# Reordering the start of the expert units around the last row codes, with more filler between row codes, in a one-core hybrid layer kernel

## What is computed

```python
def hierarchical_moe(h, w_rg, b_rg, w_re, b_re, w_gate, w_up, w_down):
    # top-1 of 4 groups, then top-2 of the 4 experts in it
    grp_prob = softmax(t @ w_rg + b_rg);  grp_p, grp_idx = top_k(grp_prob, 1)
    in_group = the 4 logits (t @ w_re + b_re) of that group
    top_logits, top_local = top_k(in_group, 2)
    weights = grp_p * softmax(top_logits)
    expert_id = grp_idx * 4 + top_local
    out[t] = sum over the two experts e:
        weight_e * ((silu(t @ w_gate[e]) * (t @ w_up[e])) @ w_down[e])
```

## Time and profile before

| | us |
|---|---|
| median of 3 runs | 668.57 |
| lowest and highest | 668.28, 669.63 |
| profiled execution, its own time | 667.52 |
| its span in the profile | 665.8 |
| mean granted clock of TensorE in it | 0.986 |
| TensorE busy | 635.4 |
| VectorE busy | 477.3 |

### The profile page before, as it was taken

How to read it: one execution, slowest core, us unless ns; L and a number is a source line. 1 busy time by engine, 2 the same in 40 slices (tenths; PEclk the granted TensorE clock), 3 DMA queues, 4 the chain that set the end, 5 groups by cost and what they waited for, 6 DMA issues and landing times.

```text
span 665.8 us, 9330 instructions
## 1 busy us (share of the span) xinstructions
PE 635.4 (95%) x3396; PEld 525.9 (79%) x3397; DVE 477.3 (72%) x808; ACT 393.6 (59%) x670; POOL 171.3 (26%) x216
## 2 busy tenths in 40 slices
PE   7999999968899999999999998999999999999985
PEld 6788878756688898888888886788888888888863
DVE  5778995367622534425664658899999999999877
ACT  7448584246635142244342463388899888998753
POOL 7000007995000000000000000234747546556100
PEclk9999999998999999999999999799999999999998
DMA  9556535203422222222325954268687876985673
GB/s 279 189 168 191 128 80 156 66 6 79 128 64 64 64 63 64 64 64 74 116 67 202 388 195 159 56 199 276 207 284 242 277 278 219 295 260 174 234 272 127
DMA packets 76960, 108.51 MB, mean 163 GB/s; under 512 B 31863, under 2 KB 54464, under 8 KB 76786
## 3 DMA queue, kind: packets, MB, share of 16 engines
q1 hardware_dynamic: 64320, 99.76, 46.4%
q0 software_dynamic: 12480, 8.11, 4.1%
q10 hardware_dynamic: 114, 0.04, 0.0%
HBM read 123.90 MB, written 20.98 MB: 218 GB/s over the span
## 4 chain that ended last, share of the span: by engine, by line
PE 85%; DVE 8%; DMA 2%; ACT 2%; issue 1%; SPq 0%; POOLq 0%; DVEq 0%; ACTq 0%
PE bank L1748 22%; PE bank L1750 22%; PE bank L1749 22%; PE bank L2201 3%; DMA expert_rows<-expert_rows_hbm 1%; PE bank L1816 1%; PE bank L1998 1%; PE bank L1988 1%; DVE rank_onehot L1586 1%; ACT w_hi L810 1%; DVE probs L1319 1%; DVE y_T L1718 1%; PE bank L2119 1%; DMA x_T<-in_x 1%; PE bank L2217 1%
## 5 line engine op out<-in xcount | busy, mean ns | idle before, releaser
L1748 PE MATMUL bank<-h_hi,w_hi 128*128 128x512 f32 x288 | 117.7, 409 | 0.0
L1750 PE MATMUL bank<-h_hi,w_lo 128*128 128x512 f32 x288 | 113.0, 392 | 0.0
L1749 PE MATMUL bank<-h_lo,w_hi 128*128 128x512 f32 x288 | 112.7, 391 | 0.0
L1466 DVE TENSOR_TENSOR gate_up_lo<-ew_raw,gate_up_hi 128x1024 fp32r<-128x1024 f32 x92 | 108.4, 1218 | 1.8 <-ACT gate_up_hi L1018 1.8
L1135 DVE TENSOR_TENSOR w_lo<-w_raw,w_hi 128x2048 fp32r<-128x2048 f32 x26 | 59.8, 2300 | 52.1 <-ACT w_hi L810 52.1
L742 POOL DMA_INDIRECT unit_tokens<-ffn_rows,row_index x23 | 27.8, 1207 | 266.1 <-DVE row_index L1594 255.1
L1018 ACT ACTIVATE gate_up_hi<-ew_raw 128x1024 fp32r<-128x1024 f32 x92 | 92.1, 1051 | 0.9 <-DMA ew_raw<-in_w_up,extra_weight_rows 0.9
L1748 PE MATMUL bank<-gate_up_hi,unit_in_hi 128*128 128x512 f32 x184 | 75.9, 413 | 0.2 <-DVE unit_in_lo L1620 0.2
L1750 PE MATMUL bank<-gate_up_hi,unit_in_lo 128*128 128x512 f32 x184 | 72.1, 392 | 0.0
L1749 PE MATMUL bank<-gate_up_lo,unit_in_hi 128*128 128x512 f32 x184 | 71.9, 391 | 0.0
L1748 PEld LDWEIGHTS bank<-h_hi,w_hi 128*128 128x128 f32 x288 | 54.5, 189 | 12.0 <-issue 2.2
(11 more groups left out here) (396 smaller groups left out, 1300.3 us busy)
## 6 DMA issues: line engine op xcount, KB each, us to landing
w_raw<-in_w_in SPq DMA_DIRECT2D x16, 1024.0 KB, 5.2
ew_raw<-in_w_gate SPq DMA_DIRECT2D x32, 512.0 KB, 6.1
ew_raw<-in_w_up SPq DMA_DIRECT2D x32, 512.0 KB, 6.3
ew_raw<-in_w_down SPq DMA_DIRECT2D x32, 512.0 KB, 5.3
expert_rows_hbm<-sub_product SPq DMA_DIRECT2D x16, 256.0 KB
w_raw<-in_w_out SPq DMA_DIRECT2D x4, 1024.0 KB, 5.1
expert_rows<-expert_rows_hbm SPq DMA_DIRECT2D x8, 512.0 KB, 7.2
x_T<-in_x SPq DMA_DIRECT2D x4, 512.0 KB, 5.0
```

What stands on the lines that cost most here:

```text
L1466: dve.tensor_tensor(dst, eraw[slot][:, :], hi.bitcast(F32), ALU.subtract).then_inc(elo_done, 1)
L1748: pe.matmul(out_ap, lhs_hi, rhs_hi, start=first, stop=False)
L1749: pe.matmul(out_ap, lhs_hi, rhs_lo, start=False, stop=False)
L1750: return pe.matmul(out_ap, lhs_lo, rhs_hi, start=False, stop=last)
```

## The change

TensorE: the filler now stands between the row codes, six ahead of batch 0, six ahead of batch 1, two ahead of batch 2 and one ahead of batch 3 (with the twelve ahead of the rank counts the filler grows from 18 to 27 matmuls). The transposes of unit 0 come ahead of the row codes of batch 4, and the first half of unit 0's products comes ahead of the transposes of unit 1 and of that of the slot weights. VectorE: the low part of unit 0's rows comes ahead of the slot weights and of the row indices of batch 4; `extra_units` is cut in two, `extra_experts` (up to the weight rows) ahead of `split_in_lo(1)` and `extra_ranks` (with `one_hots(5)` at its end) after it. The instructions are otherwise the same, and ScalarE's, GpSimd's and SyncE's orders are not touched.

```diff
--- before.py
+++ after.py
@@ -452,6 +452,7 @@
             return ps[4 * ((j + 1) % 2) + r]
 
         EARLY = 5
+        GAP_FILL = (6, 6, 2, 1)
 
         def code_units(b):
 
@@ -1604,16 +1605,6 @@
             row_ids(2)
             one_hots(4)
             row_ids(3)
-            dve.wait_ge(choice_exp, GD_OUT)
-            link(dve.tensor_reduce(gsm[:, :], gex[:, :, :], AX.X, ALU.add))
-            link(dve.reciprocal(gp[:, :], gsm[:, :]))
-            dve.wait_ge(choice_exp, ED_OUT)
-            link(dve.tensor_scalar(w12[:, 0, :], dif[:, :], 1.0, None, ALU.add))
-            link(dve.reciprocal(w12[:, 0, :], w12[:, 0, :]))
-            link(dve.tensor_tensor(w12[:, 0, :], w12[:, 0, :], gp[:, :], ALU.mult))
-            dve.tensor_tensor(w12[:, 1, :], w12[:, 0, :], dif[:, :], ALU.mult).then_inc(choice_step, 1)
-            row_ids(4)
-
             def split_in_lo(u):
                 for h in range(2):
                     dve.wait_ge(xs_hi_done, 2 * u + h + 1)
@@ -1621,7 +1612,18 @@
                                             xs_hi[u % 2][:, 4 * h:4 * h + 4, :].bitcast(F32), ALU.subtract)
                 ins.then_inc(xs_lo_done, 1)
 
-            def extra_units():
+            def slot_weights():
+
+                dve.wait_ge(choice_exp, GD_OUT)
+                link(dve.tensor_reduce(gsm[:, :], gex[:, :, :], AX.X, ALU.add))
+                link(dve.reciprocal(gp[:, :], gsm[:, :]))
+                dve.wait_ge(choice_exp, ED_OUT)
+                link(dve.tensor_scalar(w12[:, 0, :], dif[:, :], 1.0, None, ALU.add))
+                link(dve.reciprocal(w12[:, 0, :], w12[:, 0, :]))
+                link(dve.tensor_tensor(w12[:, 0, :], w12[:, 0, :], gp[:, :], ALU.mult))
+                dve.tensor_tensor(w12[:, 1, :], w12[:, 0, :], dif[:, :], ALU.mult).then_inc(choice_step, 1)
+
+            def extra_experts():
 
                 link(dve.tensor_copy(cnt[:, :], ps[6][:, TT * NE:TT * NE + NE]))
                 link(dve.tensor_tensor(over[:, :, :], bc_last(cnt[:, :], 3), bc_mid(tile_n[:, :], NE), ALU.is_gt))
@@ -1632,6 +1634,9 @@
                 link(dve.tensor_reduce(pex[:, :], past[:, :, :], AX.X, ALU.add))
                 dve.scalar_tensor_tensor(wix[:, :, :], bc_last(pex[:, :], 4), 2.0 * P, bc_mid(wbase[:, :], OVER),
                                          ALU.mult, ALU.add).then_inc(choice_step, 1)
+
+            def extra_ranks():
+
                 link(dve.tensor_tensor(obase[:, :], ends[:, :], ovn[:, :], ALU.subtract))
                 link(dve.tensor_scalar(obase[:, :], obase[:, :], float(P), 1.0 - P, ALU.mult, ALU.add))
                 r3 = rank.rearrange("p (t e) -> p t e", t=TT)
@@ -1659,8 +1664,13 @@
                 dve.tensor_tensor(l_oh[i][:, :, :], bc_mid(row_f[:, :], TT), bc_last(l_col[:, i, :], P), ALU.is_equal)
 
             split_in_lo(0)
+            slot_weights()
+            row_ids(EARLY - 1)
             dve.memset(zq[:, OVER:, :], 0.0)
-            for u in range(UNITS + 1):
+            extra_experts()
+            split_in_lo(1)
+            extra_ranks()
+            for u in range(1, UNITS + 1):
                 if u:
                     dve.wait_ge(gsilu, u)
                     if u >= 3:
@@ -1670,8 +1680,6 @@
                     split_expert_lo(KIND_G, u + 1)
                 if u + 1 < UNITS:
                     split_in_lo(u + 1)
-                if u == 0:
-                    extra_units()
                 if u:
                     if u < UNITS:
                         split_expert_lo(KIND_D, u - 1)
@@ -2186,8 +2194,8 @@
                                             ovid[c // TT][:, c % TT, 0:3], start=c == 0, stop=c == 2 * TT - 1)
                 ins.then_inc(ids_ps, 1)
 
-            keep_busy(6)
-            for b in range(EARLY):
+            for b, fill in enumerate(GAP_FILL):
+                keep_busy(fill)
                 row_codes(b)
 
             def unit_in(u):
@@ -2233,12 +2241,17 @@
                 ins.then_inc(dn_ps, 1)
 
             unit_in(0)
-            for u in range(UNITS):
+            row_codes(EARLY - 1)
+            pe.wait_ge(elo_done, place(KIND_U, 0)[2])
+            pe.wait_ge(xs_lo_done, 1)
+            gate_up(0, range(0, KT // 2))
+            unit_in(1)
+            pe.wait_ge(choice_step, WEIGHTS_SET)
+            pe.transpose(ps[1][0:2 * TT, 0:P], w12[:, :, :].rearrange("p k t -> p (k t)"), ident[:, :]).then_inc(tt_ps, 1)
+            gate_up(0, range(KT // 2, KT))
+            for u in range(1, UNITS):
                 if u + 1 < UNITS:
                     unit_in(u + 1)
-                if u == 0:
-                    pe.wait_ge(choice_step, WEIGHTS_SET)
-                    pe.transpose(ps[1][0:2 * TT, 0:P], w12[:, :, :].rearrange("p k t -> p (k t)"), ident[:, :]).then_inc(tt_ps, 1)
                 if u == 1:
                     pe.wait_ge(choice_exp, WEIGHTS_COPIED)
                 if 1 <= u <= 4:
@@ -2248,11 +2261,9 @@
                 if u >= 2:
                     pe.wait_ge(hid_done, u - 1)
                 gate_up(u, range(0, KT // 2))
-                if u:
-                    hidden_f(u - 1)
+                hidden_f(u - 1)
                 gate_up(u, range(KT // 2, KT))
-                if u:
-                    down(u - 1)
+                down(u - 1)
             hidden_f(UNITS - 1)
             down(UNITS - 1)
```

## The result

Nine runs each: the changed kernel's median is 674.13 us (672.02 to 675.53), that of the kernel before 669.63 us (668.28 to 671.41). The ratio is **1.0065**, 95% interval 1.0048 to 1.0081: slower by about 4.4 us. I had forecast no change, 668.6 us, with 670.4 as the upper end of the range.

What follows compares the result with a forecast made beforehand. It took TensorE, gapless from batch 5 on, as the bound; the better clock and earlier start (about 1.2 us) became a wait for VectorE's one-hot, sum 0.0 us on the median 668.57: 668.6 us, range 667.3 to 670.4.

Steps and rivals of the forecast that it cites:

- What bounds the kernel: Expert phase: TensorE runs without a gap for 199 us from batch 5's row codes, so their start sets the end.
- Filler costs nothing: Ahead of batches 1 to 3: nine more filler matmuls fit TensorE's waits, costed at nothing, at most 0.1 us.
- Whether the clock holds has no row: From 418 to 426 us: full clock taken as held with the new filler and earlier transposes.
- rival B: Before batch 5: clock falls all the same, low until 425.2, three products slow; plus 1.6 us, 670.2; chance 0.22.
- Rival C: Clock falls in the new wait ahead of batch 5, 1.7 to 3.4 us lost, 670.3 to 672.0; chance 0.09.
- Unit 1's transposes and VectorE's chain: Ahead of batch 5: transposes end 2.3 us later, VectorE idles 0.8 us, batch 5 starts at 432.0 against 432.02.
- The gather: Unit 0's rows: land 4.3 us after issue by the trace; the skill's fit estimated 3.2 and was not used.
- The Trainium skill's second failure mode: Around batch 5: short idles between matmul groups make the clock swing; by this rule the time would be rival B's.
- Rival D: Faster: other runs lose time to a longer low clock under unit 0's products, which the change regains; 667.2; chance 0.16.

Runs made afterwards that it cites:

- order_alone: The changed kernel without filler between the row codes, only the six matmuls ahead of batch 0; ratio 1.0054 to the kernel before.
- late_filler: The changed kernel with six filler matmuls added ahead of batch 5, behind unit 2's transposes; ratio 1.0045 to the kernel before.
- filler_alone: The kernel before with only the change's filler (6, 6, 2, 1), every order as before; ratio 1.0003.
- turn1_first: The changed kernel with unit 1's transposes put back ahead of unit 0's products; ratio 0.9998 to the kernel before.
- held_clock: Changed kernel, filler 6, 6, 5, 5 between codes, 2 ahead of unit 0's transposes, 8 behind batch 4, 6 ahead of batch 5; ratio 1.0012 to before.
- freed_order_held: turn1_first with VectorE's slot weights ahead of unit 0's low part, ranks ahead of unit 1's low part, and filler 6, 6, 4, 4; ratio 0.9991 to before.
- held_both_ends: freed_order_full with unit 1's low part back ahead of the ranks and three filler matmuls ahead of batch 5; ratio 0.9983 to the kernel before.
- freed_order_full: freed_order_held with four more filler matmuls between batch 4 and unit 1's transposes; ratio 0.9995 to the kernel before.
- old_order_held: The kernel before, in its own order, with 6, 6, 5, 5, 2 filler matmuls ahead of batches 0 to 4; ratio 0.9994.

## Why the prediction was wrong

*What bounds the kernel*: right for this change, too strong as it stood. Every trace runs from unit 3's transposes on in the same steps, unit for unit within 0.05 us, up to the step ahead of the last unit's. That one took 9.4 us in the kernel before, the changed kernel, order_alone and late_filler, and 9.9 to 10.8 in the other nine traces, filler_alone (10.6) and turn1_first (10.6) among them, with a wait of TensorE of 0.3 to 1.2 us in it. So "as long as before whatever happens ahead of it" does not hold to better than 1.5 us; what brings that wait on was not tried. Between the kernel before and the changed one the start of batch 5 set the end, with the clock just behind it.

*Filler costs nothing*: right for this amount of it (filler_alone, 1.0003); the larger amount of held_clock delays the codes by 1.25 us.

*"Whether the clock holds has no row ... so I take it as held"*: **this is the step that failed.** I took nine more wide matmuls for enough since the trace showed low clocks only where wide work was all but absent, and so I priced a fall at nothing in the sum. With 6, 6, 2, 1 the clock fell about 5 us after batch 0 in every order, as with none; 6, 6, 4, 4 held it until 8.7 us after (freed_order_held), and with filler over the later waits too (held_both_ends) it held throughout.

*The size of rival B*: the mechanism was named and mis-sized. I put its end at 425.2 "as now", and so three products at the lower clock and plus 1.6 us. But the time at which the clock comes back isn't a constant of the kernel. In the kernel before, the low stretch held 3.66 us of unbroken transposes; in the new order it held eight transposes, row codes and a wait of 1.26 us, and all twelve products ran at 0.43 us each: 5.3 us where my B had 3.5. Where the clock fell about 5 us after batch 0, the stretch was 6.8 us in every kernel whose 16 transposes stand ahead of the products, and 10.2 in each that has twelve products between them. The term measured 3.3 us, not 1.6. Why the stretch ended when it did is not shown.

*Rival C* came on top of B with 1.4 us. I had treated the two as alternatives, one or the other; they share their cause, a TensorE without wide work, and happened together. Its price was near my lower one of 1.7.

*Unit 1's transposes and VectorE's chain*: right in size and place. They end behind the twelve products, batch 5 hangs on them by 5.25 us, VectorE idles ahead of them (3.35 us, since the products were slow), and undoing this one move removes the loss.

*The gather* landed as the row said and not as the Trainium skill's fit (DMA: Bandwidth & Descriptors, Anatomy of one DMA): unit 0's transposes in the changed kernel wait for it, at the row of 421.99, and the chain that ended last (start, length) has it from its issue on:

```profile
417.81 4.14 DMA unit_tokens<-ffn_rows,row_index
```

4.1 us, where the fit gives an estimate of 3.2.

*The Trainium skill's second failure mode* (TensorE: Matmul & The Clock Gate, A second HAM failure mode), by which frequent short idles between groups of matmuls make the clock swing, had the better of my reading of the rows: the clock did swing, down, up and down again, without any idle as long as the 5.33 us of the earlier trace rows. The second fall came with the wait of 1.50 us and went with it (late_filler). Ahead of the first the idles add up to 0.64 us in 7, with row codes between the wide groups; which of the two brought it down no run here separates.

*Rival D* had nothing for it: the two traces in the old order and with little filler (before and filler_alone) have the same 6.8 us of low clock here, and the traces differ ahead of batch 0 and in the step ahead of the last unit's transposes. (Its sum gives 667.2, and the range was closed at 667.3.)

## What to carry to other kernels

Ask of a reordering on TensorE at which clock the moved work will run, and cost both clocks through to the next wait. Don't take the end of a low stretch over from the trace before: here it came 6.8 us after the fall in the old order and 10.2 in the new one. Cover for a clock is worth a run of its own: here one run of the filler by itself would have shown that it did nothing. And follow what hangs on the piece that is moved back (here unit 1's transposes, and through VectorE the next row codes), not what hangs on the piece that comes forward.

## What was not expected of the hardware

- The clock can fall while TensorE is nearly always busy: in the changed kernel it was busy for 6.36 of the 7 us ahead of 421, with row codes of three columns between the wide matmuls. In held_clock TensorE was busy for 5.18 of 6 and then for all of 6 us, with five wide matmuls between the codes, and the clock held.
- The clock fell at 433.3 in freed_order_full, with no idle over 0.89 us and TensorE busy for 7.11 of the 8 us ahead of 432.
- Low stretches of 3.4, 6.8 and 10.2 us were seen. What decides between them was not tried beyond what stands above.
- The time ahead of batch 0 differs by up to 2.7 us between traces of kernels that are the same up to there (batch 0 at 413.7 to 416.4, and 418.0 in old_order_held, which had two more low stretches of 3.4 us, near 178 and 413). The slower ones have a low clock near 42 us. In the changed kernel TensorE had no idle at all ahead of it, busy for 14.00 of the 14 us from 28 to 42, but the last of that were sixteen transposes of 8 columns (39.81, 1.95 us). The traces without the fall have the same sixteen; what decides stays open.
